# The RWKV mixer's recurrence: outputs divided and placed between the chain's steps, heads in pairs on the halves of the array

## What is computed

```python
def step(state, inp):
    r_t, w_t, k_t, v_t, a_t, b_t = inp
    sa = jnp.einsum('bhvk,bhk->bhv', state, a_t)
    state = (state * w_t[:, :, None, :] + sa[..., None] * b_t[:, :, None, :]
             + v_t[..., None] * k_t[:, :, None, :])
    return state, jnp.einsum('bhvk,bhk->bhv', state, r_t)

state0 = jnp.zeros((b_, RW_HEADS, RW_HEAD_DIM, RW_HEAD_DIM), F32)
_, y = lax.scan(step, state0, xs)
y = group_norm_heads(jnp.moveaxis(y, 0, 1), ln_g, ln_b, RW_LN_EPS)
```

## Time and profile before

| | us |
|---|---|
| median of 3 executions (2582.74, 2587.19, 2588.51) | 2587.19 |
| profiled execution, its own time | 2581.14 |
| its span (first to last instruction) | 2579.3 |
| TensorE busy | 2387.4 (93%) |
| VectorE busy | 1451.9 (56%) |
| ScalarE busy | 901.0 (35%) |
| GpSimd busy | 104.5 (4%) |
| mean granted TensorE clock | 0.957 |

### The profile page before, as it was taken

The page is one execution under the profiler, slowest core; times in us unless marked ns, Lnnn a source line. Parts: engine busy times, 40 slices in busy tenths (PEclk is TensorE's granted clock), DMA queues, the critical chain, the costliest instruction groups (busy, mean ns, idle before and its releaser), DMA issues.

```text
span 2579.3 us, 38071 instructions
## 1 busy us (share of the span) xinstructions
PE 2387.4 (93%) x15268; PEld 2045.8 (79%) x15268; DVE 1451.9 (56%) x2265; ACT 901.0 (35%) x1411; POOL 104.5 (4%) x90
## 2 busy tenths in 40 slices
PE   6999899999898899999998798789999999888998
PEld 3643678888666699999997586679989999777997
DVE  4588464444347356666655742356666665535665
ACT  3223432222224334443442310244354444324433
POOL 0000000000011000000011030000000000000000
PEclk9999999999999999999999986899999998899999
DMA  7666222222130245555533100225545553222553
GB/s 292 236 250 245 81 74 98 91 98 90 58 114 18 90 155 182 177 178 180 181 121 109 57 1 1 90 91 189 185 147 179 181 177 123 66 98 90 188 186 116
DMA packets 93984, 340.68 MB, mean 132 GB/s; under 512 B 10272, under 2 KB 12448, under 8 KB 93600
## 3 DMA queue, kind: packets, MB, share of 16 engines
q1 hardware_dynamic: 92528, 333.42, 38.3%
q10 hardware_dynamic: 1328, 5.51, 0.6%
HBM read 337.83 MB, written 1.05 MB: 131 GB/s over the span
## 4 chain that ended last, share of the span: by engine, by line
PE 87%; DVE 6%; ACT 4%; DMA 1%; issue 1%; POOL 1%; POOLq 0%; SPq 0%; DVEq 0%; ACTq 0%
PE ps L509 19%; PE ps L510 19%; PE ps L511 19%; PE ps L888 2%; PE ps L683 2%; PE ps L487 2%; PE ps L614 2%; DMA ring<-weights 1%; PE ps L521 1%; PE ps L875 1%; PE ps L767 1%; PE ps L522 1%; PE ps L1101 1%; PE ps L526 1%; PE ps L532 1%
## 5 line engine op out<-in xcount | busy, mean ns | idle before, releaser
L1776 DVE TENSOR_TENSOR WS<-ring,WS 128x1024 fp32r<-128x1024 f32 x463 | 565.4, 1223 | 415.9 <-ACT WS L1314 415.6
L1314 ACT CAST WS<-ring 128x1024 fp32r<-128x1024 f32 x463 | 482.6, 1044 | 624.0 <-PE ps L511 526.2
L509 PE MATMUL ps<-HS,WS 128*128 128x256 f32 x1888 | 535.4, 284 | 0.0
L510 PE MATMUL ps<-HS,WS 128*128 128x256 f32 x1888 | 535.1, 283 | 0.0
L511 PE MATMUL ps<-HS,WS 128*128 128x256 f32 x1888 | 535.0, 283 | 0.0
L509 PEld LDWEIGHTS ps<-HS,WS 128*128 128x128 f32 x1888 | 363.5, 193 | 0.0
L510 PEld LDWEIGHTS ps<-HS,WS 128*128 128x128 f32 x1888 | 363.4, 193 | 0.0
L511 PEld LDWEIGHTS ps<-HS,WS 128*128 128x128 f32 x1888 | 363.3, 192 | 0.0
L509 PE MATMUL ps<-HTS,WS 128*128 128x256 f32 x960 | 273.2, 285 | 3.7 <-DVE HTS L1835 3.7
L510 PE MATMUL ps<-HTS,WS 128*128 128x256 f32 x960 | 272.7, 284 | 0.0
L511 PE MATMUL ps<-HTS,WS 128*128 128x256 f32 x960 | 272.7, 284 | 0.0
(11 more groups left out here) (375 smaller groups left out, 3535.6 us busy)
## 6 DMA issues: line engine op xcount, KB each, us to landing
ring<-weights SPq DMA_DIRECT2D x633, 512.0 KB, 3.3
con<-const ACTq DMA_DIRECT2D x1, 2304.0 KB, 10.0
X<-xs ACTq DMA_DIRECT2D x1, 2048.0 KB, 8.6
X<-mem ACTq DMA_DIRECT2D x1, 1024.0 KB, 6.3
y<-X SPq DMA_DIRECT2D x4, 256.0 KB, 2.3
vecs<-vec SPq DMA_DIRECT2D x1, 311.5 KB, 7.2
con<-const SPq DMA_DIRECT2D x1, 130.0 KB, 8.4
```

The source lines that it names most:

```text
L509: pe.matmul(dst, w[0][:, cut], upper, start=first, stop=False, skip_group_check=True)
L510: pe.matmul(dst, w[0][:, cut], lower, start=False, stop=False, skip_group_check=True)
L1314: act.copy(WS[:, split % HALVES, 0, :], ring[:, panel % RING, :]).then_inc(uppers_ready, 1)
L1776: dve.tensor_tensor(WS[:, split % HALVES, 1, :], ring[:, panel % RING, :], WS[:, split % HALVES, 0, :].bitcast(F32), ALU.subtract).then_in ...
```

## The change

It touches TensorE's list in three places and VectorE's in one. The instructions' number and shapes stay as they are.

- Score products: heads come in pairs, `BF` of both heads, then `KF` of both. One step is counted for the pair, and a pair waits for the masks of the second head of the pair that had its banks.
- The chain's state products: `BT` of both heads of a pair, then `KTM` of both.
- Outputs: divided into `y_values`, `y_updates` and `y_states`, each over pairs `first` to `last`, and placed between the chain's steps. Half 0 is added up in banks 6 and 7, half 1 in banks 0 and 1. There is no wait on `rw_y0` any more.
- VectorE: both halves' copies to `YR` stand behind the last chunk.

```diff
--- before.py
+++ after.py
@@ -1078,17 +1078,18 @@
             pe.wait_ge(dve_done, at("dve", "rw_kkn"))
             for t in range(2):
 
-                for h in range(8):
-                    u, m, lo = t * 8 + h, h // 2, lo_of(h)
-                    bank = 4 + h % 4
+                for m in range(4):
+                    u = t * 8 + 2 * m
                     if u >= 4:
-                        pe.wait_ge(dve_done, at("dve", f"rw_mm{u - 4}"))
-                    ar = AR[lo:lo + 64, m, :, t * P:(t + 1) * P]
-                    pe.matmul(ps[:, bank, 0:T].rearrange("p (x t) -> p x t", x=2), BF[lo:lo + 64, m, t * P:(t + 1) * P], ar,
-                              start=True, stop=True, skip_group_check=True)
-                    s.step(pe.matmul(ps[:, bank, T:2 * T].rearrange("p (x t) -> p x t", x=2),
-                                     KF[lo:lo + 64, m, t * P:(t + 1) * P], ar, start=False, stop=True,
-                                     skip_group_check=True).then_inc(pe_done, 1), f"rw_mm{u}")
+                        pe.wait_ge(dve_done, at("dve", f"rw_mm{u - 3}"))
+                    for at_col, keys in ((0, BF), (T, KF)):
+                        for x in range(2):
+                            rows, bank = slice(64 * x, 64 * x + 64), 4 + (2 * m + x) % 4
+                            ins = pe.matmul(ps[:, bank, at_col:at_col + T].rearrange("p (x t) -> p x t", x=2),
+                                            keys[rows, m, t * P:(t + 1) * P], AR[rows, m, :, t * P:(t + 1) * P],
+                                            start=(at_col == 0), stop=True, skip_group_check=True)
+                    s.step(ins.then_inc(pe_done, 1), f"rw_mm{u + 1}")
+                    plan["pe", f"rw_mm{u}"] = s.n
 
                 for n in range(RW_LEVELS):
                     for q in range(2):
@@ -1132,47 +1133,85 @@
                 s.step(ins.then_inc(pe_done, 1), f"rw_ta{t}")
                 pe.wait_ge(act_done, at("act", f"rw_tv{t}"))
 
-            for ch in range(4):
+            y_at = lambda t, x, m, a, b: ps[64 * x:64 * x + 64, (6 if t == 0 else 0) + x, m * P + a:m * P + b]
+
+            def y_values(t, first, last):
+
+                for m in range(first, last):
+                    for x in range(2):
+                        h = 2 * m + x
+                        pe.matmul(y_at(t, x, m, 0, P), VT[:, t, h * 64:(h + 1) * 64], MR[:, t * 8 + h, 1, :], start=(m == 0),
+                                  stop=False, skip_group_check=True)
+
+            def y_states(ch, first, last):
+
+                t, a = ch // 2, 64 * (ch % 2)
+                for m in range(first, last):
+                    for x in range(2):
+                        rows = slice(64 * x, 64 * x + 64)
+                        ins = pe.matmul(y_at(t, x, m, a, a + 64), SK[rows, ch, m, :], AR[rows, m, 1, ch * 64:(ch + 1) * 64],
+                                        start=False, stop=True, skip_group_check=True)
+                return ins
+
+            def y_updates(t, first, last):
+
+                for m in range(first, last):
+                    for x in range(2):
+                        h = 2 * m + x
+                        ins = pe.matmul(y_at(t, x, m, 0, P), UB[:, t, h, :], MR[:, t * 8 + h, 0, :], start=False, stop=True,
+                                        skip_group_check=True)
+                return ins
+
+            def u_products(ch):
+
+                lo = 64 * (ch % 2)
+                for h in range(8):
+                    kl = lo_of(h)
+                    ins = pe.matmul(ps[lo:lo + 64, 2 + h % 2, (h // 2) * 64:(h // 2 + 1) * 64],
+                                    TAT[kl:kl + 64, h // 2, ch * 64:(ch + 1) * 64], SK[kl:kl + 64, ch, h // 2, :],
+                                    start=True, stop=True, skip_group_check=True)
+                s.step(ins.then_inc(pe_done, 1), f"rw_u{ch}")
+
+            def s_products(ch):
+
                 t, lo = ch // 2, 64 * (ch % 2)
-                if ch:
-                    pe.wait_ge(act_done, at("act", "rw_ta1"))
-                    pe.wait_ge(dve_done, at("dve", f"rw_s{ch}"))
-                    for h in range(8):
-                        kl = lo_of(h)
-                        ins = pe.matmul(ps[lo:lo + 64, 2 + h % 2, (h // 2) * 64:(h // 2 + 1) * 64],
-                                        TAT[kl:kl + 64, h // 2, ch * 64:(ch + 1) * 64], SK[kl:kl + 64, ch, h // 2, :],
-                                        start=True, stop=True, skip_group_check=True)
-                    s.step(ins.then_inc(pe_done, 1), f"rw_u{ch}")
-                pe.wait_ge(dve_done, at("dve", f"rw_u{ch}"))
-                if ch < 3:
-                    for h in range(8):
-                        kl = lo_of(h)
-                        dst = ps[kl:kl + 64, 4 + ch % 2, (h // 2) * 64:(h // 2 + 1) * 64]
-                        pe.matmul(dst, BT[lo:lo + 64, t, h * 64:(h + 1) * 64], UB[lo:lo + 64, t, h, :], start=True,
-                                  stop=False, skip_group_check=True)
-                        ins = pe.matmul(dst, KTM[lo:lo + 64, t, h * 64:(h + 1) * 64], VT[lo:lo + 64, t, h * 64:(h + 1) * 64],
-                                        start=False, stop=True, skip_group_check=True)
-                    s.step(ins.then_inc(pe_done, 1), f"rw_s{ch + 1}")
-                if ch % 2 == 0:
-                    continue
-
-                if t:
-                    pe.wait_ge(dve_done, at("dve", "rw_y0"))
-                for h in range(8):
-                    u, m, kl = t * 8 + h, h // 2, lo_of(h)
-                    bank = 6 + h % 2
-                    dst = lambda a, b: ps[kl:kl + 64, bank, m * P + a:m * P + b]
-                    pe.matmul(dst(0, P), VT[:, t, h * 64:(h + 1) * 64], MR[:, u, 1, :], start=True, stop=False,
-                              skip_group_check=True)
-                    ins = pe.matmul(dst(0, P), UB[:, t, h, :], MR[:, u, 0, :], start=False, stop=(t == 0),
-                                    skip_group_check=True)
-                    for cc in (2 * t, 2 * t + 1):
-                        if cc:
-                            a = 64 * (cc % 2)
-                            ins = pe.matmul(dst(a, a + 64), SK[kl:kl + 64, cc, m, :],
-                                            AR[kl:kl + 64, m, 1, cc * 64:(cc + 1) * 64], start=False, stop=True,
-                                            skip_group_check=True)
-                s.step(ins.then_inc(pe_done, 1), f"rw_y{t}")
+                for m in range(4):
+                    for first in (True, False):
+                        for x in range(2):
+                            h, kl = 2 * m + x, 64 * x
+                            cut = slice(h * 64, (h + 1) * 64)
+                            keys = (BT if first else KTM)[lo:lo + 64, t, cut]
+                            vals = UB[lo:lo + 64, t, h, :] if first else VT[lo:lo + 64, t, cut]
+                            ins = pe.matmul(ps[kl:kl + 64, 4 + ch % 2, m * 64:(m + 1) * 64], keys, vals, start=first,
+                                            stop=not first, skip_group_check=True)
+                s.step(ins.then_inc(pe_done, 1), f"rw_s{ch + 1}")
+
+            y_values(0, 0, 2)
+            pe.wait_ge(dve_done, at("dve", "rw_u0"))
+            s_products(0)
+            pe.wait_ge(act_done, at("act", "rw_ta1"))
+            y_values(0, 2, 4)
+            pe.wait_ge(dve_done, at("dve", "rw_s1"))
+            u_products(1)
+            y_values(1, 0, 2)
+            y_states(1, 0, 2)
+            pe.wait_ge(dve_done, at("dve", "rw_u1"))
+            s_products(1)
+            y_states(1, 2, 4)
+            y_updates(0, 0, 2)
+            pe.wait_ge(dve_done, at("dve", "rw_s2"))
+            u_products(2)
+            s.step(y_updates(0, 2, 4).then_inc(pe_done, 1), "rw_y0")
+            pe.wait_ge(dve_done, at("dve", "rw_u2"))
+            s_products(2)
+            y_values(1, 2, 4)
+            y_states(2, 0, 2)
+            pe.wait_ge(dve_done, at("dve", "rw_s3"))
+            u_products(3)
+            y_states(2, 2, 4)
+            y_states(3, 0, 4)
+            pe.wait_ge(dve_done, at("dve", "rw_u3"))
+            s.step(y_updates(1, 0, 4).then_inc(pe_done, 1), "rw_y1")
             pe.wait_ge(dve_done, at("dve", "rw_u3"))
             group_norm("rw", YR, blk, WSQ, lambda q: ("dve", "rw_y1"))
             out_tiles("m0", lambda k: ("dve", f"yb{k - 4}" if k >= 4 else f"ya{k}"))
@@ -2305,12 +2344,12 @@
                     dve.wait_ge(dve_done, s.n)
                     s.step(dve.tensor_tensor(SK[:, ch + 1, :, :], ps[:, 4 + ch % 2, 0:T].rearrange("p (m v) -> p m v", m=4),
                                              SKP, ALU.add).then_inc(dve_done, 1), f"rw_s{ch + 1}")
-                if ch % 2:
-                    dve.wait_ge(pe_done, at("pe", f"rw_y{t}"))
-                    for x in range(2):
-                        half = slice(64 * x, 64 * x + 64)
-                        s.step(dve.tensor_copy(YR[half, :, t * P:(t + 1) * P],
```

(7 more changed lines are left out.)

## The result

| | before | changed |
|---|---|---|
| median of 4 runs each, us | 2584.97 (2581.53 to 2588.51) | 2553.55 (2551.96 to 2556.07) |
| profiled execution, us | 2581.14 | 2552.67 |
| its span, us | 2579.3 | 2550.9 |
| mean granted clock | 0.957 | 0.966 |

The ratio is 0.9876 (95% interval 0.986 to 0.9892): 31.4 us faster, where 19.7 were forecast.

The account below looks back on a forecast made before the run. TensorE's own queue was taken to bound the kernel. Paired outputs moved into the chain's waits save 19.7 us, other terms 0: 2581.14 - 19.7 = 2561.4 for the profiled execution, median 2567.5, range 2560 to 2575.

Parts of the forecast that it names:

- What bounds the stage: From about 1472 to 1606 us: TensorE's own queue, where outputs stand between the chain's steps.
- The walk at 1.2 GHz: TensorE's queue followed block by block through the chain: final copies start at 1586.5 instead of 1606.29, 19.8 us less.
- the fifth gap: Wait ahead of updates 3, filled with four values and four states; filler put 0.7 us longer than the wait.
- the first rival: Clock comes back inside the stage because paired 128x64 products fill the array: 5 us more saved, 2562.5; chance 0.14.
- Score products at 0, between 0 and +1.2: Pairing the score products costs nothing because VectorE's masks set the pace; at most 0.3 us for each of four pairs.
- State products at 0: Pairing the chain's state products changes nothing, since the halves overlap already; bounds -0.1 and +0.1 us.
- Copies of the first half beside the last products: VectorE's two copies go behind update 3 and lie beside the last output products; otherwise they cost up to 1.4 us.
- Behind the stage: Group norm moves as a block and no later transfer takes the gain back; 0 us, between -1.8 and +1.8.
- The bound of 1.8 us on group norm's first products: L982's four products at the lower clock take 3.62 us; with the clock up, 1.8 us less.
- rivals 2 and 4: Outputs' halves do not overlap, 2576, chance 0.04; each alternation between halves drains the array, 2603 at c = 0.19, chance 0.02.
- rival 3: A shape change between long blocks costs more than 0.19 us, up to 0.33: 2570 to 2572; chance 0.10.

Follow-up runs that it names:

- k3: Changed kernel with a memset and four reciprocals on VectorE ahead of the chain's first copies, TensorE having nothing to do meanwhile; median 2574.15 us, ratio 0.9946.
- k10: The changed kernel run once more, unchanged, for a second trace; 2555.63 us, ratio 0.9887.
- k8: Kernel before with the changed kernel's paired score products and nothing else; median 2584.12 us over 12 runs, ratio 0.9991.
- k6: Kernel before with 15 more 128x128x512 products whose results nothing reads, ahead of the chain, behind its blocks and among the outputs; median 2579.72 us, ratio 0.9977.
- k2: Changed kernel with each block of outputs issued one half of the array after the other instead of alternating; median 2557.58 us, ratio 0.9874.
- k5: Changed kernel with score products and state products head by head as before, outputs as changed; median 2555.95 us, ratio 0.988.
- k7: Changed kernel with three of VectorE's four output copies moved to ScalarE; median 2554.93 us, ratio 0.9872.
- k9: k7 run again, in one call with the changed kernel; 2552.67 us, ratio 0.9873.
- k11: Changed kernel with the first half's update products moved from around the third update products to behind the last states; median 2560.33 us, ratio 0.9897.

## Why the prediction was wrong, point by point

- **What bounds the stage: right.** TensorE's queue held the outputs beside the chain, and the gain came out of that place.
- **The walk at 1.2 GHz: right.** It gave 18.7 us from the first state products to the last outputs, and 19.8 saved. k3, at a clock of 0.53, shows 17.89 and 20.5 for the order alone; with the last block priced at 0.50 as well, the estimate is 18.6 and 19.8. (By the walk's own times the filler of the fifth gap is 0.8 us longer than the wait, not 0.7; the 2.9 us on the chain holds.)
- **The clock: the step that failed.** The walk took 0.50 for the whole stage because the earlier trace rows have it so, and the first rival, that it comes back, had a chance of 0.14. I read the low clock as a property of the place. The runs show 1.00 through the chain in the changed kernel and its repeat k10, and price the term that the sum had at 0 at 6.4 us, where the rival had 5. The old order stayed at 0.50 in k8 as in the kernel before; with whole-array products among the outputs it ran at 1.00 (k6). In the changed kernel's trace the clock fell neither in the inverse's end nor in the chain. In k2, k5, k7, k9 and k11 it had fallen ahead of the chain, at the end of the inverse, and came back, which is the rival in its own words.
- **The clock ahead of the chain: 1.0 us in the trace (3.28 to 2.31), and not the change's doing as far as the runs tell.** k7 and k9 issue the same products up to the last block of outputs and have 3.18 and 3.19 there. They get it back behind the chain, where L982 to L888 takes 16.85 us instead of 18.55.
- **The rival's own price was too small.** It allowed 3 us for waits no longer hidden at 2.4 GHz. The rows show idle times of 0.26 and 0.16 us. VectorE's additions run beside a nearly full queue at either clock.
- **The argument against that rival was too narrow.** It rested on L1130, 2 us of paired products that did not lift a low clock. In k2, k7 and k9 the same products, with a block of values behind them, stood ahead of a clock that came back. What went before counts as well: the same instructions stayed at 1.00 in the changed kernel and ran at 0.53 in k3, behind a gap.
- **Score products at 0, between 0 and +1.2: wrong sign.** VectorE's pace hid nothing and cost nothing; the term came through the clock in the second inverse, -2.9 us in the changed kernel's trace, of which -1.4 goes with the score pairs in k8, and k5 without them has 91.65. Neither size is shown in whole times.
- **State products at 0: right** (k5, 0.1 us). **Copies of the first half beside the last products: right but for 0.3 us**, since L982 starts 1.88 us behind the last output's result instead of 1.59.
- **Behind the stage: right.** Group norm moved as a block (18.51 and 18.55 us), and nothing was given back over 953 us. The bound of 1.8 us on group norm's first products was real though not used here: from L982 to L888 it is 16.85 us in k2, where the clock is up for L982, 1.7 less.
- **Rivals 2, 3 and 4: refuted.** A block of 16 passes on 128x64 takes 1.09 us at 1.00, so the halves overlap, against rivals 2 and 4. Against rival 3, k3's block of values at 0.50 (1590.73) stands 1.05 us ahead of the next shape: 0.85 of streaming and 0.20 for the change, where the walk had 0.19.

Sum by measured terms: order -20.5, clock in the stage -6.4, clock ahead of it -1.0, second inverse -2.9, a start 2.2 later: -28.6, against -28.5 between the two profiles. Without the start's shift it is 30.8 by these stages, near the 31.4 between the medians. Of that, 2.5 us (1.0 ahead of the chain and 1.5 in the second inverse) belong to no edit that a run shows.

The two rules. The Trainium skill, "TensorE: Matmul & The Clock Gate", Part 3, has a weight load overlap running matmuls only when its row group differs; the traces disagree here, L1131 and L1161 with 16 passes in 1.09 us on one set of rows. Part 1 of the same page, that sustained busy time releases the half rate, would have given the better forecast, yet not for its reason: 11.70 us busy of 11.70 stayed at 0.50 in the kernel before, and 10.77 of 11.30 stayed at 1.00 after the change.

What stays open is what exactly the clock follows. The fall ahead of the chain came while TensorE was busy with the end of the inverse, in some traces and not in others with the same products. The runs show which work stood ahead of each fall and rise, in this kernel. They don't separate the share of the array in use from the length of gaps, and I didn't try to.

## What to carry to other kernels

Where a stage runs at the lower clock, do not cost a reordering at that clock alone: price it at both levels, and ask whether the work being moved (half the array in use, waits left bare) is itself what goes with the low level. Products on half of TensorE's array go in blocks of one shape over both halves, into the waits of the dependent chain beside them; here the pairing took 17.6 us off the stage and the placing 9.35 more. A run of the new order entered behind a forced gap tells the order's share from the clock's in one kernel.

## What the runs showed of the hardware

- The same 248 matmul records took 11.3 us at 1.00 (changed kernel) and 17.9 at 0.53 (k3), behind a gap of 14 us. L1131 had run at 0.50 ahead of the gap in k3 already (1.97 us); k7, with 1.97 there too and no gap, took 11.3 from its first state products (1575.98) to its last outputs (1586.19 and 1.09).
- With the `ta` products at 0.50 in both, the clock returned within the first state products in k2, with the new outputs, and stayed at 0.50 for 48 us in k8, with the old ones, though TensorE was busy for 11.50 of 11.50 us of their first stretch (1578.9 to 1590.4).
- Fifteen products that nothing reads made the kernel before 0.2% faster (k6, ratio 0.9977), though they take some 16 us (15 times 1.07).
- Two heads on one half followed by two on the other overlap without being alternated (0.66 us for 8 passes in either order), and four followed by four only in part (k2, 1.58 instead of 1.09 us for 16 passes).
- An f32 product over 512 columns on the whole array stands in the trace as two passes, and put between two heads' outputs it cost 1.07 us at 2.4 GHz (k6).
